# Three-pass split products for the odd output, the branch projections and the mixer output, and a residual in quarters

## What is computed

```python
# odd layer
mixed = stick_breaking_attention(q, k, v) @ odd_w_out[i]      # 256 x 1024 @ 1024 x 1024
x = x + mixed
hn = rmsnorm(x, ffn_norm[layer])
# mixer of the second block
merged = jax.nn.sigmoid(z_g) * (o_g @ w_proj_gla) + jax.nn.sigmoid(z_m) * (o_m @ w_proj_moba)
return merged @ w_out                                         # both projections 512 -> 1024, w_out 1024 x 1024
```

## Time and profile before

| what | us |
|---|---|
| three runs | 1457.07, 1457.13 (median), 1459.61 |
| the profiled execution: its own time | 1459.65 |
| its span, first to last instruction | 1457.9 |
| mean granted TensorE clock | 0.937 |
| TensorE busy / weight loads busy | 1245.9 / 948.8 |
| VectorE busy / ScalarE busy | 638.8 / 425.5 |
| HBM read | 340.32 MB |

### The profile page before, as it was taken

How to read it: one execution, slowest core, us unless ns; L and a number is a source line. 1 busy time by engine, 2 the same in 40 slices (tenths; PEclk the granted TensorE clock), 3 DMA queues, 4 the chain that set the end, 5 groups by cost and what they waited for, 6 DMA issues and landing times. The chain is left out here.

```text
span 1457.9 us, 19669 instructions
## 1 busy us (share of the span) xinstructions
PE 1245.9 (85%) x8096; PEld 948.8 (65%) x8096; DVE 638.8 (44%) x975; ACT 425.5 (29%) x559; POOL 24.6 (2%) x83
## 2 busy tenths in 40 slices
PE   5899999999998999999989899998776767758663
PEld 4785899998984999998887876873331323313321
DVE  8964465557666465556445434550110101101012
ACT  5363243324554333335363312311100100101000
POOL 2110000000000000000000000000000000000000
PEclk9999999999999999999996999999878879988887
DMA  9513265554433365556450434686999999999993
GB/s 262 92 61 116 87 216 199 194 195 149 162 122 121 117 226 179 173 173 211 143 174 30 161 137 145 226 327 264 422 420 422 422 421 422 422 421 422 422 422 137
DMA packets 137143, 343.92 MB, mean 236 GB/s; under 512 B 9826, under 2 KB 99036, under 8 KB 112500
## 3 DMA queue, kind: packets, MB, share of 16 engines
q1 hardware_dynamic: 135276, 337.96, 61.8%
q0 software_dynamic: 1696, 4.99, 1.9%
q10 hardware_dynamic: 104, 0.02, 0.0%
HBM read 340.32 MB, written 2.62 MB: 235 GB/s over the span
## 5 line engine op out<-in xcount | busy, mean ns | idle before, releaser
L1108 PE MATMUL ps<-HT_hi,piece_hi 128*128 128x256 f32 x1088 | 309.8, 285 | 8.8 <-DVE HT_lo L1725 6.9
L1109 PE MATMUL ps<-HT_lo,piece_hi 128*128 128x256 f32 x1088 | 307.7, 283 | 0.0
L1110 PE MATMUL ps<-HT_hi,piece_lo 128*128 128x256 f32 x1088 | 307.5, 283 | 0.0
L1734 DVE TENSOR_TENSOR piece_lo<-ring,piece_hi 128x2048 fp32r<-128x2048 f32 x104 | 235.1, 2286 | 97.6 <-ACT piece_hi L733 97.0
L733 ACT ACTIVATE piece_hi<-ring 128x2048 fp32r<-128x2048 f32 x104 | 196.3, 1910 | 229.3 <-PE ps L1110 150.8
L1108 PEld LDWEIGHTS ps<-HT_hi,piece_hi 128*128 128x128 f32 x1088 | 208.4, 192 | 12.3 <-issue 10.4
L1109 PEld LDWEIGHTS ps<-HT_lo,piece_hi 128*128 128x128 f32 x1088 | 208.6, 192 | 0.8
L1110 PEld LDWEIGHTS ps<-HT_hi,piece_lo 128*128 128x128 f32 x1088 | 208.4, 192 | 0.0
L1553 PE MATMUL ps<-ring,arena 128*32 128x512 f32 x992 | 137.4, 711 | 71.4 <-DMA ring<-in_w_exp_up_dram 70.3
L1553 PEld LDWEIGHTS ps<-ring,arena 128*32 128x32 f32 x992 | 36.8, 128 | 165.9 <-issue 164.6
L1574 PE MATMUL ps<-ring,arena 128*32 128x512 f32 x496 | 82.9, 813 | 58.9 <-DMA ring<-in_w_exp_down_dram 58.9
(11 more groups left out here) (419 smaller groups left out, 1652.8 us busy)
## 6 DMA issues: line engine op xcount, KB each, us to landing
ring<-in_w_exp_gate_dram SPq DMA_DIRECT2D x64, 1024.0 KB, 19.2
ring<-in_w_exp_down_dram SPq DMA_DIRECT2D x62, 1024.0 KB, 15.9
ring<-in_w_exp_up_dram SPq DMA_DIRECT2D x60, 1024.0 KB, 16.2
ring<-in_ffn_w_gate_dram SPq DMA_DIRECT2D x22, 1024.0 KB, 5.5
ring<-in_ffn_w_up_dram SPq DMA_DIRECT2D x22, 1024.0 KB, 5.4
...
```

Of the source, the lines that this page charges most:

```text
L1108: pe.matmul(out, sh, mh, start=start, stop=False, skip_group_check=True)
L1109: pe.matmul(out, sh, ml, start=False, stop=False, skip_group_check=True)
L1110: return pe.matmul(out, sl, mh, start=False, stop=stop, skip_group_check=True)
L1734: ve.tensor_tensor(piece_lo[k % RING][:, :], ring[:, k % RING, :], piece_hi[:, h % HI_SLABS, :].bitcast(F32), ALU.subtract).then_inc(split, 1)
```

## The change

- odd_out, proj_g, proj_m and mix_out (12 pieces) join the split names and go through `three_passes`.
- The tiles sb0_o, sb1_o, moba_o, g_oT are now emptied by both engines in turn: ACT writes the high part over MT (`out_hi_part`), then DVE the low part (`out_lo_part`) and raises `emptied`; TILE_PLAN says "v" for both tiles of each. The merged tokens get a high part by ACT (`merged_hi`) and a low part by DVE (`merged` is raised after it); mix_out's piece n waits for merged n + 1 only.
- The output products, split or plain, and the down products of both feed-forwards run column half outside, k tile inside; `mix_full` and `residual` are raised for each quarter (block, half), and the residual is added quarter by quarter. ACT's norm_sq waits for its block's two quarters.
- `norm` for the raw norms 1 to 4 and for 7 transposes bank by bank (both blocks' two column tiles), and waits for the quarter that it reads.
- Splits of later pieces (ffn1 3, z6, z7, c_q 1) are issued later in ACT's or DVE's program.

Cut to its core, indentation reduced (left out: declarations, semaphores, the same reordering in the down products, TILE_PLAN):

```diff
@@ -68,7 +68,9 @@
 SPLIT_NAMES = (["ffn0"] + [f"odd_{c}{half}" for half in range(2) for c in "qkv"]
-               + ["ffn1", "g_q", "g_k", "g_v", "g_r", "m_q", "m_k", "m_v", "z", "mem_k", "c_q", "mem_v"])
+               + ["odd_out", "ffn1", "g_q", "g_k", "g_v", "g_r", "m_q", "m_k", "m_v", "z", "proj_g", "proj_m", "mix_out",
+                  "mem_k", "c_q", "mem_v"])
+SPLIT_TILES = ["sb0_o", "sb1_o", "moba_o", "g_oT"]
 SPLIT_PIECES = [FIRST_PIECE[name] + i for name in SPLIT_NAMES for i in range(dict(STREAM)[name])]
@@ -273,6 +276,9 @@
 HT_hi, HT_lo = sb_over("HT_hi", [P, KT, T], ring_byte, PIECE * RING), sb_over("HT_lo", [P, KT, T], HT_byte, 0)
+MT_hi = sb_over("MT_hi", [P, KT, T], MT_byte, 0)
+odd_lo = [sb_over(f"odd_lo{i}", [P, 4, T], arena_byte, 2048 * i) for i in range(2)]
+mixer_lo = sb_over("mixer_lo", [P, KT, T], arena_byte, 3072)
 HTm_hi, HTm_lo = sb_over("HTm_hi", [P, KT, T], arena_byte, 9216), sb_over("HTm_lo", [P, KT, T], arena_byte, 7168)
@@ -696,6 +703,11 @@
     act.activation(dst, b, ACT.Copy, scale=scale).then_inc(emptied["a"], 1)
+def out_hi_part(name, i, first):
+    b = full_tile(act, name, i).rearrange("p (a b) -> p a b", a=2)
+    act.activation(MT_hi[:, first:first + 2, :], b, ACT.Copy).then_inc(out_hi, 1)
@@ -879,16 +891,24 @@
         piece_hi_part("odd_v1", 0)
+    else:
+        for n in (2, 3):
+            piece_hi_part("odd_out", n)
     act.wait_ge(probs, ATT[name] + 1)
...
     pt_odd(name, A1, 384)
-    empty(name + "_o", 1, MT[:, 4 * half + 2:4 * half + 4, :], 2)
-for n in range(4):
+    for i in range(2):
+        out_hi_part(name + "_o", i, 4 * half + 2 * i)
+    if half == 0:
+        for n in (0, 1):
+            piece_hi_part("odd_out", n)
+for n in range(3):
     piece_hi_part("ffn1", n)
...
 norm_sq(3, X)
+piece_hi_part("ffn1", 3)
 glu(1)
@@ -949,16 +969,36 @@
 pt_odd("moba", PT2, 384)
-empty("moba_o", 1, MT[:, 6:8, :], 2)
-empty("g_oT", 1, MT[:, 2:4, :], 2)
-gates((6, 7))
+piece_hi_part("proj_g", 0)
+for i in range(2):
+    out_hi_part("moba_o", i, 4 + 2 * i)
+for i in range(2):
+    out_hi_part("g_oT", i, 2 * i)
+piece_hi_part("proj_g", 1)
+gates((6,))
+piece_hi_part("proj_m", 0)
+gates((7,))
+piece_hi_part("proj_m", 1)
 norm_sq(5, mem_raw)
-for name in ("mem_k", "c_q"):
-    for i in range(2):
-        piece_hi_part(name, i)
+def merged_hi(i):
+    act.wait_ge(summed, i + 1)
+    act.activation(HT_hi[:, 2 * i:2 * i + 2, :], HT[:, 2 * i:2 * i + 2, :], ACT.Copy).then_inc(summed_hi, 1)
+piece_hi_part("mix_out", 0)
+piece_hi_part("mix_out", 1)
+merged_hi(0)
+merged_hi(1)
+piece_hi_part("mix_out", 2)
+merged_hi(2)
+merged_hi(3)
+piece_hi_part("mix_out", 3)
+for i in range(2):
+    piece_hi_part("mem_k", i)
+piece_hi_part("c_q", 0)
 norm_columns_split(5, HTm_hi)
 norm_sq(6, X)
+piece_hi_part("c_q", 1)
 empty("mem_k", 1, c_k[:, 2:4, :], 2)
@@ -1022,16 +1062,19 @@
     pe.transpose(banks[0][:, 0:P], ident[:, :], ident[:, :])
-for tb in range(2):
-    if n in RAW_NORMS or n == 7:
-        pe.wait_ge(residual, 2 * RESIDUALS_BEFORE[n] - 1 + tb)
-    else:
+raw = n in RAW_NORMS or n == 7
+order = [(tb, kt) for tb in range(2) for kt in range(KT)]
+if raw:
+    order = [(tb, 2 * i + kk) for i in range(4) for tb in range(2) for kk in range(2)]
+for tb, kt in order:
+    if raw and kt % 4 == 0:
+        pe.wait_ge(residual, 4 * RESIDUALS_BEFORE[n] - 3 + 2 * tb + kt // 4)
+    elif not raw and kt == 0:
         pe.wait_ge(normed, 2 * n + tb + 1)
-    for kt in range(KT):
-        c = (kt % 2) * T + tb * P
-        ins = pe.transpose(banks[kt // 2][:, c:c + P], (X if n in RAW_NORMS or n == 7 else XN)[:, tb, kt * P:(kt + 1) * P], ident[:, :])
-        if tb == kt % 2 == 1:
-            ins.then_inc(bank_full, 1)
+    c = (kt % 2) * T + tb * P
+    ins = pe.transpose(banks[kt // 2][:, c:c + P], (X if raw else XN)[:, tb, kt * P:(kt + 1) * P], ident[:, :])
+    if tb == kt % 2 == 1:
+        ins.then_inc(bank_full, 1)
 for _ in range(fillers[1]):
@@ -1083,19 +1126,58 @@
         for tb in range(2):
-            for kk in range(2):
-                kt = 2 * n + kk
-                for half in range(2):
+            for half in range(2):
+                for kk in range(2):
+                    kt = 2 * n + kk
                     ins = pe.matmul(ps[:, 4 + 2 * tb + half, :], MT[:, kt, tb * P:(tb + 1) * P],
...
                                     stop=(kt == 2 * of - 1), skip_group_check=True)
-            if n == of - 1:
-                ins.then_inc(mix_full, 1)
+                if n == of - 1:
+                    ins.then_inc(mix_full, 1)
         if n < of - 1:
...
+def output_part_split(name, pieces, first, of, hi, lo, ready=None):
+    for n, i in enumerate(pieces, first):
+        if ready is not None:
+            pe.wait_ge(ready, n + 1)
+        wh, wl = split_piece(FIRST_PIECE[name] + i, 2)
+        for tb in range(2):
+            t = slice(tb * P, (tb + 1) * P)
+            for half in range(2):
+                c = slice(half * 512, (half + 1) * 512)
+                for kk in range(2):
+                    kt = 2 * n + kk
+                    ins = three_passes(ps[:, 4 + 2 * tb + half, :], (hi[:, kt, t], lo(kt)[:, t]),
+                                       (wh[:, kk, c], wl[:, kk, c]), kt == 0, kt == 2 * of - 1)
+                if n == of - 1:
+                    ins.then_inc(mix_full, 1)
+        if n < of - 1:
+            ins.then_inc(piece_used, 1)
+def odd_lo_of(kt):
+    return odd_lo[kt // 4][:, kt % 4, :]
+def projection_split(name, hi, lo):
+    for i in range(2):
+        wh, wl = split_piece(FIRST_PIECE[name] + i, 4)
+        for half in range(2):
+            b = open_tile(pe, name, 2 * i + half)
+            for f in range(2):
+                c = slice((2 * half + f) * P, (2 * half + f + 1) * P)
+                for kt in range(4):
+                    ins = three_passes(b[:, f * T:(f + 1) * T], (wh[:, kt, c], wl[:, kt, c]),
+                                       (hi[:, kt, :], lo[:, kt, :]), kt == 0, kt == 3)
+                    if i == 1 and half == f == kt == 0:
+                        ins.then_inc(piece_used, 1)
+            ins.then_inc(bank_full, 1)
+    pe.wait_ge(bank_full, full_count(name, 3))
+    pe.nop().then_inc(piece_used, 1)
 def output_done(name):
-    pe.wait_ge(mix_full, 2 * (RESIDUAL_NO[name] + 1))
+    pe.wait_ge(mix_full, 4 * (RESIDUAL_NO[name] + 1))
     pe.nop().then_inc(piece_used, 1)
@@ -1428,23 +1510,10 @@
 feature_major_split("z", 2, first=6)
-feature_major("proj_g", 2, MT[:, 0:4, :], 4)
-feature_major("proj_m", 2, MT[:, 4:8, :], 4)
-pe.wait_ge(merged, 4)
-for i in range(4):
-    w = piece(FIRST_PIECE["mix_out"] + i, 2)
-    for tb in range(2):
-        for kk in range(2):
-            kt = 2 * i + kk
-            for half in range(2):
-                ins = pe.matmul(ps[:, 4 + 2 * tb + half, :], HT[:, kt, tb * P:(tb + 1) * P],
-                                w[:, kk, half * 512:(half + 1) * 512], start=(kt == 0), stop=(kt == 7))
-        if i == 3:
-            ins.then_inc(mix_full, 1)
-    if i < 3:
-        ins.then_inc(piece_used, 1)
-pe.wait_ge(mix_full, 2 * (RESIDUAL_NO["mix_out"] + 1))
-pe.nop().then_inc(piece_used, 1)
+projection_split("proj_g", MT_hi[:, 0:4, :], mixer_lo[:, 0:4, :])
+projection_split("proj_m", MT_hi[:, 4:8, :], mixer_lo[:, 4:8, :])
+output_part_split("mix_out", range(4), 0, 4, HT_hi, lambda kt: HT_lo[:, kt, :], merged)
+output_done("mix_out")
 norm(5, wait=False)
@@ -1661,19 +1730,25 @@
+def out_lo_part(name, i, first, lo):
+    b = full_tile(ve, name, i).rearrange("p (a b) -> p a b", a=2)
+    ve.wait_ge(out_hi, 2 * SPLIT_TILES.index(name) + i + 1)
+    ve.tensor_tensor(lo, b, MT_hi[:, first:first + 2, :].bitcast(F32), ALU.subtract).then_inc(emptied["v"], 1)
 def add_residual(r):
     for tb in range(2):
-        ve.wait_ge(mix_full, 2 * r + tb + 1)
         for half in range(2):
+            ve.wait_ge(mix_full, 4 * r + 2 * tb + half + 1)
             xs = X[:, tb, half * 512:(half + 1) * 512]
...
                 ins = ve.tensor_tensor(xs, xs, ps[:, 4 + 2 * tb + half, :], ALU.add)
-        ins.then_inc(residual, 1)
-        ve.wait_ge(residual, 2 * r + tb + 1)
+            ins.then_inc(residual, 1)
+    ve.wait_ge(residual, 4 * r + 4)
@@ -2024,6 +2099,9 @@
     piece_lo_part("odd_q1", 1)
+else:
+    for n in (0, 1):
+        piece_lo_part("odd_out", n)
 b = full_tile(ve, f"odd_v{half}", 0).rearrange("p (a c) -> p a c", a=2)
@@ -2043,13 +2121,18 @@
         qk("odd_k", ok, 1)
+    else:
+        piece_lo_part("odd_out", 2)
     pt_even(name, A1, 384)
-    empty(name + "_o", 0, MT[:, 4 * half:4 * half + 2, :], 2)
-for n in range(4):
+    for i in range(2):
+        out_lo_part(name + "_o", i, 4 * half + 2 * i, odd_lo[half][:, 2 * i:2 * i + 2, :])
+piece_lo_part("odd_out", 3)
+for n in range(3):
     piece_lo_part("ffn1", n)
...
 norm(3, X)
+piece_lo_part("ffn1", 3)
 glu(1)
@@ -2172,18 +2255,28 @@
     by_root("z", i, sig[i])
-    piece_lo_part("z", 2 + i)
+piece_lo_part("z", 6)
 pt_even("moba", PT2, 384)
```

(48 more changed lines are left out.)

19 lines of the change are left out of this document (8 added, 11 removed).

## The result

| | before | after |
|---|---|---|
| median of the runs, us | 1458.16 (4 runs, 1457.07 to 1459.61) | 1446.63 (4 runs, 1443.79 to 1448.40) |
| profiled execution: time / span | 1459.65 / 1457.9 | 1446.55 / 1444.8 |
| mean granted clock | 0.937 | 0.924 |
| busy: TensorE / weight loads | 1245.9 / 948.8 | 1245.5 / 965.6 |
| busy: VectorE / ScalarE | 638.8 / 425.5 | 669.1 / 451.9 |

A forecast was written before the change was run, and what follows sets the result against it. TensorE bounds the touched stretches; the DMA-bound experts start when it arrives. Norms 2.85 + 0.35, odd layer 2.1, mixer 9.8 make 15.1 us, less 2.0 for the clock: 1446.55 profiled, 1444.0 median; range 1440.5 to 1449.5.

The forecast's parts named there:

- rival (2): Mixer: a second clock fall between 820.77 and 825.15, costing 1.7 to 3.4 us more, about 1446.5; chance 0.16.
- Products: odd_out, projections and mix_out in three passes instead of plain: 5.2 us saved in each, together 15.6 of TensorE time.
- Norms: Norms by quarters: 0.95 us saved at each of norms 1, 2 and 4, 2.85 together; about 0.35 at norm 7.
- Odd layer: Second odd half: 2.1 us saved in all, while idle time before sb1's transposes grows from 1.46 to 4.1.
- Mixer: z6 starts 1.85 us later, then projections and mix_out run on without long waits; 9.8 us saved.
- I expect 1.2 GHz once in sb1: Clock falls to half rate once, after the 4.1 us idle time in sb1; cost taken as 2.0 us.
- my list of idle times followed by 0.50: Earlier trace's low clocks: after idle times of 2.84 and 3.42 us, and a 3.35 us stretch with 0.63 busy.
- Covers: Mixer splits on DVE ready 7.6 us before TensorE needs them; next late would be DVE, by 1.5 us of cover.
- rival (3): Mixer: DVE and ACT become the bound, the saving falls to about 6 us, 1451; chance 0.07.
- Rival (5): Experts: the saving vanishes because their first 18 pieces arrive no sooner, 1457 us; chance 0.03.
- rival (4): Clock stays low through dense passes after both new gaps, two stretches costing 27.3 us against 15.1: 1469; chance 0.04.

The follow-up runs named there:

- the fillers: The kernel after, with unread transposes in TensorE's idle times: 30 after the second odd_out piece, 12 before each mixer wait (moba_o, g_oT); 1442.42 us, ratio 0.9899.
- the late waits: The kernel after, with TensorE's waits for split head-output tiles moved to where a product reads them; 1438.77 us, ratio 0.9881 to the kernel before.

## Why the prediction was right, and where it was not

The median was predicted at 1444.0 and came at 1446.6, in the range, and nearest to rival (2), the second fall in the mixer, which I had priced at 1446.5 and given 0.16. Of the difference of 2.6 us, 1.0 is the median that I started from (1457.13 in three runs, 1458.16 in four), and 1.45 the second fall. That the profiled execution had the 1446.55 that I worked out for it is luck: the parts of the change moved it by 11.7 and not 13.1.

- **Products: right.** Passes cost 0.238 us in odd_out (11.44 for 48) and 0.229 in mix_out (22.00 for 96), where I took 0.233. The 288 passes from z6 on took 37.07 with 3.4 us of them at half clock, so 0.123 at full. From z6 to the end of the projections that is 35.4 us for the 35.25 reckoned (which has half a microsecond too much, for 836.9 and 192 passes of 0.120 give 859.9 and not 860.4). The mixer's start came as reckoned: z6 1.75 late before the clock, where I had 1.85.
- **Norms: mis-sized.** 0.85, 0.80 and 0.80 at norms 1, 2 and 4 (gaps of 3.93, 4.04 and 4.04 to 3.08, 3.24 and 3.24), not 0.95. Norm 7 gave 0.49 (3.81 to 3.32), not 0.35. Together 2.94 for 3.20. The step is ACT's start on bank 0: 1.24 us after the products' end at norm 2, where I had 1.05.
- **Odd layer: right.** From product to product 128.27 us became 128.19: 0.08 saved. I had 2.1 less 2.0 for the clock; the fillers put the clock's part at 1.66. The new idle time was 4.01 for the 4.1 of the text, the low clock behind it 3.4 us.
- **Mixer: the step that failed.** 9.8 was foreseen, 8.64 came, and 10.09 with the clock held by fillers. What failed is "I expect 1.2 GHz once in sb1": the sentences on idle times of 1.46 and 1.56 that do no harm took each gap alone, while here 1.53 and 1.69 around 1.07 us of work were enough. Which of the two did it, or whether it took both, no run parts: the fillers and the late waits took both away. The row that said so, 3.35 us with 0.63 of work, stood in rival (2). And my list of idle times followed by 0.50 left out a fall in the trace before, at 967.4, behind norm 7's transposes and inside the router's short products, where the only idle times were 0.41 and 1.27 us. With it, the length of a single idle time could not have been the rule:

```profile
964.65 4.49 PE L1485 MATMUL ps<-router_w,HT 128*128 128x36 f32 x32 [1.27 <-ACT HT L690]
...
967.40:974.20 6.80, 6.80 (x34) 6.80 (x34) 6.08 (x38) 0.00 (x0) 1.36 (x5) 0.50 1.00 418
```

- **Covers: right.** Mix_out's last piece had 7.9 us to spare (7.6 reckoned), norm 6 moved nothing, rival (3) had no ground: 5 us more on VectorE cost 0.3. Rival (5) fell too: the first expert product came 11.5 us earlier, and the end 13.1.
- **Slower, rival (4)**: neither new fall lasted beyond 6.8 us in any execution. Dense passes are not what ended the one in sb1: the clock is back at 451.0, among transposes and small products, and the passes start at 455.87. The one place where it stays down for 20 to 31 us is z's stretch, with short products between idle times (TensorE busy for 26.3 of 30.7 us). That these are the reason is argued, not shown.
- **Outside the change**: z's low clock was 30.7 us long and took 1.2 us more than in the execution before; start-up was 1.0 shorter, the experts' stretch 1.6. With the parts above: 2.94 + 0.08 + 8.64 - 1.2 + 1.0 + 1.6 = 13.1.

The rule that I had weighed in the Trainium skill ("TensorE: Matmul & The Clock Gate", why this matters for your kernels) against idle gaps between bursts fits both new falls and deserved more weight: they took back 3.1 us, as the fillers show. On the three-pass price the trace stays against the four passes of the Trainium skill ("FP8 and Floating Point Precision", the list on FP32): 22.00 to 27.73 is 79%, not 75%. What makes the difference no run here shows; the weight loads and the fixed cost that the prediction named were not measured apart.
